# Seven block products instead of eight for the second projection of the first FFN, in three of its four groups

## What is computed

```python
def first_block(x, ...):
    ...
        nm = rmsnorm(h, mlp_norm_g[l])
        a = jnp.square(jax.nn.relu(jnp.einsum('bsd,df->bsf', nm, w_ff1[l])))   # 1024 -> 4096
        h = h + jnp.einsum('bsf,fd->bsd', a, w_ff2[l])                         # 4096 -> 1024
    return rmsnorm(h, final_norm_g)
```

## Time and profile before

| | us |
|---|---|
| median of three runs | 1383.29 |
| lowest and highest | 1381.76, 1385.16 |
| the profiled execution, its time | 1382.6 |
| its span, first to last instruction | 1381.3 |
| TensorE busy | 1372.7 |
| ScalarE, VectorE, POOL busy | 838.9, 629.1, 211.5 |
| granted TensorE clock | 1.000 of full speed |

### The profile page before, as it was taken

The page is one execution under the profiler, slowest core; times in us unless marked ns, Lnnn a source line. Parts: engine busy times, 40 slices in busy tenths (PEclk is TensorE's granted clock), DMA queues, the critical chain, the costliest instruction groups (busy, mean ns, idle before and its releaser), DMA issues.

```text
span 1381.3 us, 17229 instructions
## 1 busy us (share of the span) xinstructions
PE 1372.7 (99%) x6682; PEld 1112.0 (81%) x6682; DVE 629.1 (46%) x1225; ACT 838.9 (61%) x1246; POOL 211.5 (15%) x259
## 2 busy tenths in 40 slices
PE   9999999999999999999999999999999999999999
PEld 6977966788888888887777878888888888888887
DVE  6055466521211212356588789975434312331341
ACT  6575666754544545666488767775566645663661
POOL 0211100111111111111211111211111111111111
PEclk9999999999999999999999999999999999999999
DMA  7976644898888888877665675768879988889885
GB/s 251 234 169 134 147 116 94 182 195 188 196 191 196 194 194 193 190 167 153 151 133 123 135 192 123 141 150 174 199 177 212 195 193 193 190 196 194 193 169 122
DMA packets 68326, 239.53 MB, mean 173 GB/s; under 512 B 7602, under 2 KB 7915, under 8 KB 68116
## 3 DMA queue, kind: packets, MB, share of 16 engines
q0 software_dynamic: 36144, 130.32, 52.3%
q1 hardware_dynamic: 31236, 106.24, 24.2%
q10 hardware_dynamic: 864, 1.87, 0.4%
HBM read 236.28 MB, written 2.12 MB: 173 GB/s over the span
## 4 chain that ended last, share of the span: by engine, by line
PE 95%; DMA 2%; ACT 2%; DVE 1%; issue 0%; SPq 0%; ACTq 0%
PE bank L538 29%; PE bank L545 28%; PE bank L542 28%; PE bank L705 2%; PE bank L681 2%; PE bank L695 1%; PE bank L662 1%; DMA WL<-in_w_in 1%; PE bank L730 1%; DMA WH<-in_w_in 1%; DMA RAW<-in_w_in 1%; PE bank L713 0%; ACT WH L861 0%; PE bank L642 0%; PE bank L763 0%
## 5 line engine op out<-in xcount | busy, mean ns | idle before, releaser
L538 PE MATMUL bank<-NH,WH 128*128 128x512 f32 x1152 | 463.2, 403 | 0.3 <-ACT NH L1042 0.3
L542 PE MATMUL bank<-NL,WH 128*128 128x512 f32 x1152 | 448.2, 390 | 0.5 <-DVE NL L1272 0.5
L545 PE MATMUL bank<-NH,WL 128*128 128x512 f32 x1152 | 448.0, 390 | 0.4 <-DVE WL L1267 0.4
L861 ACT ACTIVATE WH<-RAW 128x1024 fp32r<-128x1024 f32 (+3 forms) x196 | 202.0, 1032 | 194.8 <-PE bank L545 186.6
L538 PEld LDWEIGHTS bank<-NH,WH 128*128 128x128 f32 x1152 | 216.4, 188 | 62.1 <-issue 19.3
L545 PEld LDWEIGHTS bank<-NH,WL 128*128 128x128 f32 x1152 | 216.2, 188 | 46.6 <-DVE WL L1267 0.8
L542 PEld LDWEIGHTS bank<-NL,WH 128*128 128x128 f32 x1152 | 216.7, 188 | 45.3 <-issue 2.6
L869 ACT ACTIVATE WL<-WH 128x1024 fp32r<-128x1024 f32 (+2 forms) x219 | 229.4, 1048 | 24.2 <-DMA WH<-in_w_in 19.1
L542 PE MATMUL bank<-AL,WH 128*128 128x512 f32 x432 | 168.2, 389 | 0.0
L545 PE MATMUL bank<-AH,WL 128*128 128x512 f32 x432 | 168.1, 389 | 0.0
L538 PE MATMUL bank<-AH,WH 128*128 128x512 f32 x432 | 168.1, 389 | 0.0
(11 more groups left out here) (342 smaller groups left out, 1645.0 us busy)
## 6 DMA issues: line engine op xcount, KB each, us to landing
RAW<-in_w_ff SPq DMA_DIRECT2D x64, 512.0 KB, 5.2
WL<-in_w_ff POOLq DMA_DIRECT2D x64, 512.0 KB, 8.9
WL<-in_w_in POOLq DMA_DIRECT2D x58, 512.0 KB, 7.3
RAW<-in_w_gu SPq DMA_DIRECT2D x44, 512.0 KB, 6.6
WL<-in_w_gu POOLq DMA_DIRECT2D x44, 512.0 KB, 8.7
WH<-in_w_in POOLq DMA_DIRECT2D x32, 512.0 KB, 6.5
RAW<-in_w_in SPq DMA_DIRECT2D x28, 512.0 KB, 6.8
RAW<-in_w_down SPq DMA_DIRECT2D x20, 512.0 KB, 4.9
```

What stands on the lines that cost most here:

```text
L538: e.matmul(o, a[0], a[1], start=(k == 0), stop=False)
L542: e.matmul(o, b[0], b[1], start=False, stop=False)
L545: mm = e.matmul(o, c[0], c[1], start=False, stop=(k == t.kt - 1))
L861: e.activation(WH[p % HL][:, 0:n], RAW[raw_slot[p]][:, 0:n], ACT.Copy).then_inc(*act.sig("high", p))
```

## The change

In groups 0 to 2 a unit of f2 is treated as a product of matrices of 2 x 2 blocks. The weight's blocks are A11, A12, A21, A22 (128 output features by four contraction tiles, the even or the odd ones of the eight); the activation's blocks are four contraction tiles by 256 tokens. Eight block products give the four blocks of the result. By Winograd's scheme seven are enough if sums of blocks are multiplied: S1 = A22 + A21, S2 = S1 - A11, S3 = A11 - A21, S4 = A12 + A11 - S1, and T1 to T4 likewise for the activations. Each product is four contraction tiles, three passes, 128 x 256: 12 matmuls.

- TensorE: 84 matmuls of 256 columns a unit for 48 of 512. `SEVEN` lists the products: piece, first weight column, first activation column, bank, part. Bank 0 gets four of the seven on top of each other, and VectorE adds its content to h in between, so that products 3, 4, 5 and 6 wait for earlier additions (h_part).
- Activations, in f1 of groups 0 to 2: tiles 2j and 2j+1 form a pair. VectorE makes T1 to T4 in `sums1`, ScalarE rounds 1792 columns a pair (four parts: even, even_sum, odd, odd_sum), VectorE subtracts for their low parts.
- Weights: the unit's four quarters go by two DMAs of 512 KB from SP to one of two buffers `quarters`. POOL makes S1 to S4 in five operations of 512 columns (`quarter_sums`), for units 2 and 3 of a group during the unit ahead, for units 0 and 1 during f1. ScalarE rounds them in four pieces (1024, 1024, 1024, 512 columns), VectorE subtracts for the low parts (`quarter_rests`). No negative, no accumulating DMA.
- `after`: the first five pieces of the stage behind each of these groups get their low parts by a subtraction on VectorE too.
- h: six additions of 256 columns and one of 512 a unit (`seven_out`) instead of two of 512.
- Group 3 stays as it was.

The diff, cut to its core:

```diff
+SEVEN = [(0, S, 0, 0, "even"), (0, 0, UC, 2, "even_sum"), (1, 0, 5 * UC, 1, "odd"), (2, S, 2 * UC, 0, "odd_sum"),
+         (2, 0, 6 * UC, 2, "odd"), (1, S, 4 * UC, 1, "odd_sum"), (3, 0, 3 * UC, 0, "odd_sum")]
+SEVEN_GROUPS = 3
+OPENS = (0, 1, 2, 5)
+CLOSES = (4, 2, 5, 6)
...
+PART = {"even": (0, UC), "even_sum": (UC, 2 * UC), "odd_sum": (2 * UC, 5 * UC), "odd": (5 * UC, 7 * UC)}
...
-        AH1, AL1, ft1 = rows_of("AH1", 8, F32R), rows_of("AL1", 8, F32R), two("ft1", 6)
+        AH1, AL1 = ([sb(f"{n}{j}", 7 * UC, F32R) for j in range(4)] for n in ("AH1", "AL1"))
...
+        sums1 = nc.alloc_sbuf_tensor_at("sums1", [P, 4 * UC], F32, offset=places["ft14"])[:, :]
+        quarters = [sb(f"quarters{i}", 5 * S) for i in range(2)]
+        quarters_s = sb("quarters_s", 2 * S)
...
+        after = {plan.first[u] + 4 + i: (u, i) for u in plan.sevens if u + 1 not in plan.sevens for i in range(5)}
+        firsts = [*range(ADDED), *sorted(after)]
...
+            def seven(t, n):
+                piece, w0, x0, bank, part = SEVEN[n]
+                s, g, p = plan.sevens.index(t.u), t.st[1], plan.first[t.u] + piece
+                o = FB[seven_bank(s, bank)][:, 0:UC]
+                if n == 0 and s < 2:
+                    pe.wait_ge(*(f for f in fb["free"] if f))
+                if n in OPENS and s > (n == 0):
+                    pe.wait_ge({0: ("h_part", plan.sevens[s - 2], 6), 1: ("h_part", plan.sevens[s - 1], 4),
+                                2: ("h_part", plan.sevens[s - 1], 5), 5: ("h_part", t.u, 2)}[n])
+                if n in (3, 4, 5, 6):
+                    pe.wait_ge(("h_part", t.u, {3: 0, 4: 1, 5: 2, 6: 3}[n]))
+                pe.wait_ge(high(p), low(p))
+                for j in range(4):
+                    pe.wait_ge(("pair_high", g, j, part), ("pair_low", g, j, part))
+                    w, x = slice(w0 + j * P, w0 + (j + 1) * P), slice(x0, x0 + UC)
+                    wh, wl, xh, xl = WH[p % HL][:, w], WL[p % HL][:, w], AH1[j][:, x], AL1[j][:, x]
+                    for i, (a, b) in enumerate(((wh, xh), (wh, xl), (wl, xh))):
+                        mm = e.matmul(o, a, b, start=(n in OPENS and j == 0 and i == 0),
+                                      stop=(n in CLOSES and j == 3 and i == 2), skip_group_check=True)
+                mm.then_inc(*pe.sig("seven", t.u, n))
...
+                    if plan.step(p) is not None:
+                        q = quarters[plan.sevens.index(u) % 2]
+                        act.wait_ge(plan.freed(p - HL))
+                        act.wait_ge(*[[("quarter_sum", u, "S1"), (f"quarters_1{plan.sevens.index(u) % 2}", u)],
+                                      [(f"quarters_2{plan.sevens.index(u) % 2}", u)],
+                                      [("quarter_sum", u, "S2"), ("quarter_sum", u, "S4")], [("quarter_sum", u, "S3")]][k])
+                        part = (q[:, 2 * S:4 * S], q[:, 0:2 * S], quarters_s, q[:, 4 * S:5 * S])[k]
+                        e.activation(WH[p % HL][:, 0:(S if k == 3 else 2 * S)], part, ACT.Copy).then_inc(*act.sig("high", p))
+                        continue
...
-                    e.activation(AH1[:, t.i, :], f, ACT.Copy).then_inc(*act.sig(*hi(("f1", g), t.i)))
...
+                    j = t.i // 2
+                    def rounded_part(part, x):
+                        lo_, hi_ = PART[part]
+                        e.activation(AH1[j][:, lo_:hi_], x, ACT.Copy).then_inc(*act.sig("pair_high", g, j, part))
+                    if t.i % 2 == 0:
+                        rounded_part("even", f[:, 0:UC])
+                        yield due(t, 3.5)
+                        act.wait_ge(("pair_sum", g, j, 0))
+                        rounded_part("even_sum", sums1[:, 0:UC])
+                    else:
+                        rounded_part("odd", f)
+                        yield due(t, 3.5)
+                        act.wait_ge(("pair_sum", g, j, 3))
+                        rounded_part("odd_sum", sums1[:, UC:4 * UC])
...
-                for p in range(ADDED):
+                for p in firsts:
...
-                    e.tensor_tensor(AL1[:, t.i, :], f, AH1[:, t.i, :].bitcast(F32), ALU.subtract).then_inc(*dve.sig(*lo(("f1", g), t.i)))
...
+                    def rest(part, x):
+                        lo_, hi_ = PART[part]
+                        dve.wait_ge(("pair_high", g, j, part))
+                        e.tensor_tensor(AL1[j][:, lo_:hi_], x, AH1[j][:, lo_:hi_].bitcast(F32),
+                                        ALU.subtract).then_inc(*dve.sig("pair_low", g, j, part))
+                    def difference(n, to, a, b, *waits):
+                        dve.wait_ge(*waits)
+                        e.tensor_tensor(to, a, b, ALU.subtract).then_inc(*dve.sig("pair_sum", g, j, n))
+                    yield due(t, 2.5)
+                    if t.i % 2 == 0:
+                        back = [("pair_low", g, j - 1, "odd_sum") if j else ("pair_low", g - 1, 3, "odd_sum")] if g or j else []
+                        difference(0, T1, f[:, UC:], f[:, 0:UC], ("relu_square", g, t.i), *back)
+                        rest("even", f[:, 0:UC])
+                        yield due(t, 4.5)
+                        rest("even_sum", T1)
+                    else:
+                        x1 = ft1[(t.i - 1) % 3]
+                        difference(1, T2, f[:, UC:], T1, ("relu_square", g, t.i), ("pair_sum", g, j, 0))
+                        difference(2, T3, f[:, UC:], x1[:, UC:])
+                        difference(3, T4, f[:, 0:UC], T2, ("pair_sum", g, j, 1))
+                        rest("odd", f)
+                        yield due(t, 4.5)
+                        rest("odd_sum", sums1[:, UC:4 * UC])
...
+                    def rest(i, x):
+                        n = x.shape[1]
+                        dve.wait_ge(("high", p + i))
+                        e.tensor_tensor(WL[(p + i) % HL][:, 0:n], x, WH[(p + i) % HL][:, 0:n].bitcast(F32),
+                                        ALU.subtract).then_inc(*dve.sig("low_sum", p + i))
+                    for i in (0, 1, 2, 3) if plan.sevens.index(u) % 4 == 0 else (0, 1, 3, 2):
+                        yield low_time(p + i)
+                        rest(i, (q[:, 2 * S:4 * S], q[:, 0:2 * S], quarters_s, q[:, 4 * S:5 * S])[i])
...
+                    steps = [(k, one_, first, []), (k1, two_, third, []), (k, one_, second, [0]), (k, two_, first, []),
+                             (k, two_, third, [3]), (k1, one_, second, [])]
+                    for n, (row, ts, bank, back) in enumerate(steps):
+                        yield t.v0 + SEVENTH * (n + 1) + 0.8
+                        dve.wait_ge(("seven", u, n), ("h", *before, row), *(("h_part", u, i) for i in back))
+                        e.tensor_tensor(hT[:, row, ts], hT[:, row, ts], bank, ALU.add).then_inc(*dve.sig("h_part", u, n))
...
+                    dve.wait_ge(("seven", u, 6), ("h_part", u, 5), ("h_part", u, 1))
+                    both = hT[:, k1, :].rearrange("p (n s) -> p n s", n=2)
+                    e.tensor_tensor(both, both, first.unsqueeze(1).to_broadcast([P, 2, UC]), ALU.add).then_inc(*dve.sig("h_part", u, 6))
...
-                    if p < ADDED:
+                    if p in firsts or plan.step(p) is not None:
...
+                yield times[0]
+                add("S1", S1, A22, A21, ALU.add, (f"quarters_2{s}", u), (f"quarters_1{s}", u))
+                yield times[1]
+                add("S3", A21, A11, A21, ALU.subtract, ("quarter_sum", u, "S1"))
+                yield times[2]
+                back = [("low_sum", plan.first[plan.sevens[n - 1]] + 2)] if n else []
+                add("A12 + A11", S4, A12, A11, ALU.add, *back)
+                yield times[3]
+                add("S4", S4, S4, S1, ALU.subtract, ("quarter_sum", u, "A12 + A11"))
+                yield times[4]
+                add("S2", S2, S1, A11, ALU.subtract)
...
+                for s, u in enumerate(plan.sevens):
+                    if s < 2:
+                        yield plan.start(("f1", 0)) + 2.0 + 4.0 * s
+                        sp.wait_ge(("h", "wo0", 7), ("dil_out", 3))
+                    else:
+                        p = plan.first[plan.sevens[s - 2]]
+                        yield low_time(p + 3) + 1.2
+                        sp.wait_ge(*(("low_sum", p + i) for i in (0, 1, 3)), ("quarter_sum", plan.sevens[s - 2], "S2"))
+                    src, q = A["w_ff2"][plan.units[u][2]], quarters[s % 2]
+                    e.dma_start(q[:, 0:2 * S], src[:, 0:2 * S]).then_inc(*sp.sig(f"quarters_2{s % 2}", u, by=16))
+                    e.dma_start(q[:, 3 * S:5 * S], src[:, 2 * S:4 * S]).then_inc(*sp.sig(f"quarters_1{s % 2}", u, by=16))
```

More of the change, by code:

```diff
@@ L90, in __init__ @@
         self.kt, self.cols, self.sets, self.v0, self.v1 = kt, cols, sets, v0, v1
+        self.seven = st[0] == "f2" and st[1] < SEVEN_GROUPS
 NATURAL = {"vG", "vD", "vS", "vH"}
@@ L150, in __init__ @@
         paired = {0, next(u for u, unit in enumerate(units) if unit[0] == "wo2")}
```

(50 more changed lines are left out.)

104 lines of the change are left out of this document (81 added, 23 removed).

## The result

The changed kernel took **1391.8 us** (median of 4 runs, 1391.49 to 1392.44), the kernel before 1382.5 beside it (1381.55 to 1385.16): a ratio of 1.0065, 95% interval 1.0047 to 1.0082. It is 0.65% slower, where 0.6% faster was forecast. The profiled execution has a span of 1390.2 us.

A forecast was written before the change was run, and what follows sets the result against it. TensorE, by number of matmuls times spacing, was taken as the bound. From the profiled 1382.6 us, minus 9.8 for spacing, plus 1.5 for a DMA wait, gives 1374.3, brought to the median 1375.0 us; range 1372 to 1380.5.

The forecast's parts named there:

- Part 6: POOL's weight-sum additions: 1.2 us each, hidden within a unit; cost 0 up to about 1.4 us each, even with engine exclusion.
- Part 8: DMA queues and f1's VectorE load: cost 0, no gain; the added VectorE work is hidden in free time.
- What bounds the kernel: Whole kernel: the number of TensorE matmuls times their spacing counts; other engines matter only where they make TensorE wait.
- Part 1: f2 units: 84 matmuls of 256 columns instead of 48 of 512, gaining 0.82 us a unit, 9.8 us over 12 units.
- Parts 2 to 4: f2 additions to h, VectorE's low parts, ScalarE's copies (also f1): all hidden; VectorE cover 1.0 us, cost 0.
- Part 5: Head of each group's f2 stage: slack 0.25 to 0.35 us everywhere; cost 0, up to 0.5 us a head in the range.
- rival A: Exclusion with POOL additions of 1.9 us delays product 3 in f2: 1390 us; 8% eats all the gain, 5% half.
- above 1.4 us: Failure sign for POOL's weight-sum additions: the prediction fails if one takes longer than this; 0.95 to 1.4 us expected.
- Part 7: One more POOL instruction before f1's last accumulating DMA in the first group: TensorE waits 1.5 us once, bounds 0 and 5.8.
- L: Time of the extra ISA row on POOL in the first group, taken as 5.2 us; TensorE waits L - 3.7.

The follow-up runs named there:

- Kernel 4: The changed kernel with the 60 weight-sum additions made by VectorE instead of POOL, at the same due times: 1372.4 us; 1371.1 us when measured again.
- kernel 1: The changed kernel with two fills, which read nothing in SBUF, in place of each of POOL's 60 additions (sums left out): 1372.2 us.
- kernel 2: The changed kernel with fills replacing POOL's additions only for units 0 and 1 of each group, those in f1: 1371.1 us, one run.
- kernel 3: The changed kernel with fills replacing POOL's additions only for units 2 and 3 of each group, those in f2: 1390.7 us, one run.

## Why the prediction was wrong, point by point

The gain was forecast rightly; what failed is that POOL's additions were put at no cost to VectorE in f1. Part 6 walked the exclusion through for f2 only, and Part 8 counted f1 without it. The runs showed 13.6 us of waiting at three heads in its place, and some 5 us of half clock behind them.

**What bounds the kernel; Part 1: right.** Without late operands the stage lasts 40.3 us, as forecast, with matmuls 0.12 apart. Three stages at 3.2 us less are 9.7 us, for a forecast of 9.8. Kernel 4 as a whole gains 10.4 us (1382.8 to 1372.4); of that, 0.4 is the wait of 1.0 us for a DMA in the earlier trace rows, which is 0.6 there (and gone in the change and in kernels 1 and 2).

**Parts 2 to 4: right.** Behind the head no unit waits for h or a weight; from 312.20 to 348.60 TensorE is busy in all of it.

**Part 5: wrong, by inheritance.** The head's chain was counted from an evacuation of tile 7 that starts 0.2 us after the product. That is how it stood before; in the change VectorE comes to tile 6 at 305.00, when both tiles are long done. The slack of 0.3 us was of a chain whose start had moved; in kernel 1, where it had not (tile 7 at 300.07), no head waits.

**Part 6: the size was right, the walk was too short.** POOL's addition takes 1.30 us where undisturbed (taken: 1.2; bounds 0.95 to 1.37), so rival A's slow POOL is out. Beside VectorE's work it takes up to 2.34 us, which is waiting; the sign "above 1.4 us" did not tell the two apart. The exclusion was named and bounded (each fully waits for the other), and that bound is what happened. But it was worked through for a unit of f2 alone. There it costs about nothing (kernel 3). Half of the additions stand in f1.

**Part 8, its last sentence: the step that failed.** "f1's VectorE load grows by about 2.8 us a pair and up to 1.23 a piece, of 27 us free in 43.5: hidden." It leaves out two things. POOL's ten additions in f1, 13 us, count against the same free time once the engines exclude each other. And free time of a stage is no cover for a chain: VectorE is still idle for 10.5 of the 42.6 us before the first f2 stage, but pair 0's five steps stand in a row, they meet five additions in a row, and 2.9 us (272.30 to 275.19 in kernel 1) become 8.7. With the load alone (kernels 1 and 4) the sentence holds. The rivals had the right mechanism (A), but the wrong condition (a slow POOL) and the wrong place (product 3 of units 2 and 3). That A's 1390 us comes near the 1391.8 measured is luck.

**The clock** had no term. 5 us of the 19 lost are half clock behind the pauses.

**Part 7: wrong, 1.5 us for nothing.** The row that I priced at 5.2 us took 0.36, and the last accumulating DMA was held up by ScalarE instead: issued at 285.95, not 280.2 + L. That this is near the 285.4 which L = 5.2 would give is luck. It still came in time, since it landed after 5.8 us, not 9.3; the DMA engines were busy for 0.53 of that f1 stage, before for 0.86. That the lighter traffic made it faster is not shown. TensorE's list holds no wait for it.

POOL's instruction ahead of its first addition, and the landing of that DMA:
```profile
L2103 POOLq MODIFY_POOL_CONFIG  x2: 357/358/358, 272.9 to 272.9; - x2
```
```profile
DMA to landing us min/median/max: 5.8/5.8/5.8
```

## What to carry to other kernels

In this kernel, work that went from VectorE to POOL and reads SBUF there stayed on VectorE's account wherever VectorE had two operands in SBUF: cost such a move as an exclusion, in every stage where its instructions fall and not just where its results are used. Here 60 additions cost VectorE 0.76 us each on POOL and 0.69 us on VectorE itself. If POOL must do it, place it beside operations with an operand in PSUM or where VectorE is idle, and away from chains: the same instructions at other places gave 1373 instead of 1392 us.
